# Moving the modulation sums of a transformer block's attention stage from VectorE to ScalarE and GpSimd

## The chip, the cores and the metric

The kernel runs on one core of a Trainium2 chip. The metric is the device time of one launch in microseconds; the time before is 2897.89 us, the median of three runs. The engines are named PE (TensorE), DVE (VectorE), ACT (ScalarE), POOL (GpSimd) and SP (SyncE, which here only issues transfers).

## The reference

Two transformer blocks follow each other on x of 1024 tokens by 1024 channels in float32. The change touches the first one's attention stage:

```python
cond = jax.nn.silu(c)
mod = jnp.einsum('bd,de->be', cond, w_ada[i]) + b_ada[i]
sh1, sc1, gt1, sh2, sc2, gt2 = jnp.split(mod, 6, axis=-1)
h = _rmsnorm(x, g_mix[i]) * (1.0 + sc1) + sh1
q, k, v, qi, ki, wi, cu = jnp.split(h @ w_in[i], split_at, axis=-1)
attn_out = _dsa_attention(q, k, v, qi, ki, wi)   # top 256 keys by an index score, causal
conv_out = _conformer_conv(cu, ...)              # 31 taps, layer norm, silu
x = x + gt1 * (jnp.concatenate([attn_out, conv_out]) @ w_out[i])
# then an MLP of width 4096 modulated with sh2, sc2 and gt2, and the second block
```

Each query keeps the 256 keys with the highest index score. `mod` is a vector-matrix product of a 1024-vector with a 1024 x 6144 matrix.

## The kernel before, in words

Every float32 matmul is made of three: each operand is split into a rounded high part and a low rest (`h_hi`, `h_lo`; `w_hi`, `w_lo`; `q_hi`, `q_lo`), and the products hi*hi, hi*lo and lo*hi are summed in PSUM. Weights come by SP's transfers into four buffers `raw`, in a fixed order (`slots`); a buffer is filled again once a semaphore says that its last user is done.

All engines run one list written by hand, `MICRO`, each taking from it the entries that concern it, in order. The attention stage is 64 slots: 8 query tiles `t` of 128 tokens, 8 heads each; slot `n` is 8t + head. Per slot PE makes the scores (two heads at a time), the transposes of the probabilities two slots back (`turn`) and the product with the values four slots back (`values`). DVE adds the mask to the scores and takes the row maximum (`mask`, line 1503), ACT takes the exponential (line 995) and copies the transposed probabilities out of PSUM (line 987).

The other work of the block is spread over the same slots:

- `conv`: the 31-tap depthwise convolution, as matmuls with diagonal matrices. There are 8 units of 31 taps; `UNIT_SLOTS` gives the slots in which each runs and `taps_by(n)` the taps done by slot n. POOL builds the diagonals three taps at a time (line 662), in two buffers; it waits until PE has used those of two groups earlier. PE takes three matmuls per tap (lines 2099 to 2101).
- `topk`: for query tile 4, DVE finds the 256 highest scores in 32 rounds of eight (lines 1367 and 1369).
- `sel_pass` and `sel_step`: for query tiles 5 to 7, the 256th score is found by bisection of its bits. A pass on ACT counts the scores above a candidate (three `Sign` operations with an accumulator, line 934); a step on DVE makes the next candidate from it (four operations on 3 elements, lines 1388 to 1398). The step of a pass stands one slot after it. `sel_fin` then turns the scores of a tile into a mask on DVE, in six parts, and has to be done before that tile's first slot.
- `ada`: the products for the four parts of `mod` that are used after attention. Each of 32 items takes a 128 x 1024 piece of `w_ada` in `raw`, multiplies it by a column of silu(c) and adds it to one of the sums `gate_sum` or `mlp_sum`. This is one DVE operation (line 1524, or 1527 for a part's first item without bias). `ADA_SLOTS` puts item i at slot 8i // 5. `ada_sum` counts them; it frees the `raw` buffer, and PE's `modsum` (slot 46) and `gate` (slots 57 and 58) wait for it.
- `ln_...`: the layer norm of the convolution, at slots 26 to 42 for the first half of the tokens and at slots 62 and 63 and behind the loop for the second. Its last step is `ln_silu` (line 1573).
- `split_q`: POOL's split of q, once per tile; `wsplit`: POOL's split of the first two pieces of `w_out`, at slots 60 and 62.

After slot 63 a hand-written tail follows with the last values and turns, the division by the row sums (`divide`, line 1538), `ln_silu`, the first matmuls of the output projection (`mixed`: part 0 or 1 for each of four token tiles) and the last rounding to `h_hi` and `h_lo`. There is no scheduler at run time; only the order of the list and the semaphores set what waits for what.

Of the kernel before, what the change touches and what calls it, by code (L numbers as in the profile page):

```python
# [6 lines left out]
ALU = mybir.AluOpType  # L7
ACT = mybir.ActivationFunctionType
# [8 lines left out]
NT = S // P  # L17
NK = D // P
# [5 lines left out]
NH, NKV, HD = 8, 2, 64  # L24
# [21 lines left out]
SEL_TILES = IDX_TILES[3:]  # L46
# [22 lines left out]
def build(nc, a, out):  # L69
    with ExitStack() as ctx:  # L70
        sems = {}

        def sem(name):
            if name not in sems:
                sems[name] = ctx.enter_context(nc.semaphore(name))
            return sems[name]
# [183 lines left out]
        M_OUT = len(used)  # L260
# [136 lines left out]
        TOPK_Q, TOPK_K, TOPK_LAST = 40, 52, 12  # L397
        TOPK_SLOTS = {4: range(0, 31)}
        SEL_EARLY, SEL_ROUNDS = 8, 4
        SEL_AT = {n: SEL_EARLY + k for k, n in enumerate(n for n in range(32) if n % 4 < 3)}  # L400
        FIN_SLOTS = {}
        for ti, at_slots in zip(SEL_TILES, (range(32, 38), range(39, 45), range(46, 52))):
            for part, n in enumerate(at_slots):
                FIN_SLOTS[n] = [("sel_fin", ti, part)]
        UNIT_SLOTS = (0, 6, 12, 18, 24, 34, 42, 52, 62)

        def taps_by(n):

            n = min(n, UNIT_SLOTS[-1])
            u = max(m for m in range(2 * NCC) if UNIT_SLOTS[m] <= n)  # L410
            n0, n1 = UNIT_SLOTS[u], UNIT_SLOTS[u + 1]
            return CONV_K * u + -(-CONV_K * (n - n0) // (n1 - n0))
# [6 lines left out]
        N_ADA = 4 * NK  # L419
        ADA_SLOTS = {8 * i // 5: i for i in range(N_ADA)}  # L420
        GATE_SLOTS = {46: [("modsum", 0, 0)], 57: [("gate", 0, 0), ("gate", 0, 1)], 58: [("gate", 1, 0), ("gate", 1, 1)]}
        WSPLIT_SLOTS = {60: 0, 62: 1}
        MICRO = [("split_q", 0, 0), ("split_q", 1, 0)]
        for t in range(NT):
            for i in range(0, NH, 2):
# [3 lines left out]
                last, older = ([(s // NH, s % NH) for s in (NH * t + i - d, NH * t + i - d + 1)] for d in (2, 4))  # L429
                n = NH * t + i  # L430
                taps = [taps_by(n), taps_by(n) + (taps_by(n + 2) - taps_by(n)) // 3, taps_by(n + 2)]
                for e in range(2):
# [8 lines left out]
                    if n - 1 in SEL_AT:  # L441
                        MICRO.append(("sel_step", SEL_AT[n - 1], 0))
                    if taps[e + 1] > taps[e]:
                        MICRO.append(("conv", taps[e], taps[e + 1]))
                    if n in WSPLIT_SLOTS:
# [12 lines left out]
                    if n in ADA_SLOTS:  # L458
                        MICRO.append(("ada", ADA_SLOTS[n], 0))
                    MICRO += GATE_SLOTS.get(n, [])  # L460
        assert len(SEL_AT) == SEL_PASSES - SEL_EARLY
        assert TOPK_K + TOPK_LAST == 2 * ROUNDS
        assert taps_by(NT * NH) == 2 * NCC * CONV_K
        MICRO += [("values", NT - 1, NH - 4), ("turn", NT - 1, NH - 2), ("values", NT - 1, NH - 3), ("turn", NT - 1, NH - 1),
                  ("mixed", 0, 0), ("mixed", 0, 1), ("ln_gate", 1, 0), ("values", NT - 1, NH - 2), ("values", NT - 1, NH - 1), ("divide", NT - 1, 0),
                  ("ln_silu", 1, 0)]
        MICRO += [("mixed", 0, t) for t in range(2, 4)] + [("out", NT - 1, 0)]
        MICRO += [("ln_hi", 0, 0), ("ln_lo", 0, 0), ("ln_hi", 1, 0), ("ln_lo", 1, 0)]
# [85 lines left out]
        def _(pool):  # L554
# [55 lines left out]
            for n, (kind, _, (n1, n2)) in enumerate(slots):  # L610
# [23 lines left out]
                if m == M_OUT:  # L634
# [13 lines left out]
                    for kind, t, i in MICRO:  # L648
                        tok = slice(t * P, (t + 1) * P)
                        if kind == "split_q" and t >= 2:  # L650
                            split_q(t)
# [139 lines left out]
        def _(act):  # L791
# [184 lines left out]
            for kind, t, i in MICRO:  # L976
# [20 lines left out]
                if kind == "sel_pass":  # L997
                    sel_pass(t, sel_out)
                if kind == "out":
                    u = tp_of[t, "o"]  # L1000
                    act.wait_ge(sem("tp_full"), tp_count[u])
                    s.activation(h_hi[:, 0:4, t * P:(t + 1) * P], ps[:, 4 + u % 2, :].rearrange("p (c q) -> p c q", q=P),
                                 ACT.Copy).then_inc(sem("attn_hi"), 1)
# [214 lines left out]
        def _(dve):  # L1218
# [274 lines left out]
            for kind, t, i in MICRO:  # L1493
# [18 lines left out]
                if kind == "topk":  # L1512
                    topk(t, i)
                if kind == "ada":
                    part, k = t // NK, t % NK
                    acc = (gate_sum[0], mlp_sum[0], mlp_sum[1], gate_sum[1])[part]
                    n = 2 * NK + M_OUT + t
                    dve.wait_ge(raw_in[n % 4], 16 * (n // 4 + 1))
                    if k:
                        dve.wait_ge(sem("ada_sum"), t)  # L1520
                    elif part in (0, 3):
                        dve.wait_ge(sem("gate_bias"), 32)
                    if k or part in (0, 3):
                        v.scalar_tensor_tensor(acc, raw[:, n % 4, :], csil[:, k:k + 1], acc, ALU.mult,
                                               ALU.add).then_inc(sem("ada_sum"), 1)
                    else:
                        v.tensor_scalar(acc, raw[:, n % 4, :], csil[:, k:k + 1], None, ALU.mult).then_inc(sem("ada_sum"), 1)
                if kind == "sel_step":
# [869 lines left out]
```

## Time and profile before

| what | value |
|---|---|
| median of 3 runs | 2897.89 us (2894.88 to 2903.49) |
| the profiled execution, its own time | 2897.89 us |
| its span, first to last instruction | 2896.0 us |
| PE busy | 2707.7 us, 93% |
| DVE busy | 1670.2 us, 58% |
| ACT busy | 759.5 us, 26% |
| POOL busy | 1150.2 us, 40% |
| attention stage, slots 0 to 63 | about 340 to 697 us |

Busy time is the time in which the engine has at least one instruction under way; for PE the ends of matmuls are modelled. An engine's idle time matters only where it is the one that the others wait for. The granted clock is the share of TensorE's full 2.4 GHz that it got; 0.5 is 1.2 GHz.

### The profile page before, as it was taken

The page shows a single profiled execution, that of the slowest core. Times are in us where ns is not written, and L with a number is a line of the kernel's source. Part 1 is how long each engine was busy: PE and PEld are TensorE (multiplying, and loading weights), DVE is VectorE, ACT ScalarE, POOL GpSimd, SP SyncE. Part 2 cuts the span into 40 slices and gives each one's busy share as a digit, 9 for nine tenths or more (in the row PEclk, how much of TensorE's full clock was granted, in tenths as well). Part 3 has the DMA queues.
Part 4 walks back from the last instruction along what each step waited for, and adds up shares of the span by engine and source line. Part 5 has one row for each costly group of instructions (what it writes and reads, how often), then busy time and mean ns, then how long its engine had stood idle before and what let it go on. Part 6 is the DMA issues. An engine that isn't in the chain of part 4 may idle for free.

```text
span 2896.0 us, 34615 instructions
## 1 busy us (share of the span) xinstructions
PE 2707.7 (93%) x13488; PEld 2240.6 (77%) x13488; DVE 1670.2 (58%) x2150; ACT 759.5 (26%) x1314; POOL 1150.2 (40%) x764
## 2 busy tenths in 40 slices
PE   4999988998999999999999999788799999999998
PEld 4867776887878888888876677677688888888887
DVE  6268988855475566665675782455526334444335
ACT  4235477434231001111023442222214000111002
POOL 2422464533454354354342223333364334334332
PEclk8999999999999999999999999899999999999999
DMA  6201021212311111111122110000231111111111
GB/s 217 66 12 33 30 73 51 62 34 76 106 59 42 46 58 43 44 58 38 54 73 67 43 37 15 1 1 1 78 105 59 37 51 58 36 51 58 36 51 58
DMA packets 142488, 153.33 MB, mean 53 GB/s; under 512 B 7183, under 2 KB 105252, under 8 KB 142374
## 3 DMA queue, kind: packets, MB, share of 16 engines
q1 hardware_dynamic: 136512, 141.87, 15.5%
q10 hardware_dynamic: 5862, 9.89, 0.9%
q8 instruction: 77, 1.26, 0.2%
q14 instruction: 37, 0.30, 0.0%
HBM read 143.35 MB, written 8.39 MB: 52 GB/s over the span
## 4 chain that ended last, share of the span: by engine, by line
PE 78%; DVE 12%; ACT 4%; issue 3%; POOL 1%; DMA 1%; ACTq 0%; SPq 0%; DVEq 0%; POOLq 0%
PE ps L1920 11%; PE ps L1905 11%; PE ps L1922 11%; PE ps L1921 11%; PE ps L1907 11%; PE ps L1906 11%; PE ps L2301 4%; ACT sel_out L934 2%; DVE yt L1742 2%; PE ps L2073 2%; PE ps L1996 2%; DVE yt L1731 1%; DVE score L1369 1%; DVE best L1367 1%; PE ps L2063 1%
## 5 line engine op out<-in xcount | busy, mean ns | idle before, releaser
L1905 PE MATMUL ps<-h_hi,w_hi 128*128 128x512 f32 x1472 | 585.3, 398 | 10.1 <-issue 5.6
L1906 PE MATMUL ps<-h_lo,w_hi 128*128 128x512 f32 x1472 | 575.0, 391 | 0.0
L1907 PE MATMUL ps<-h_hi,w_lo 128*128 128x512 f32 x1472 | 575.0, 391 | 0.0
L681 POOL TENSOR_TENSOR w_hi<-raw,zero 128x1024 fp32r<-128x1024 f32 x128 | 243.7, 1904 | 780.2 <-PE ps L1907 397.3
L1920 PE MATMUL ps<-w_hi,u_hi 128*128 128x512 f32 x1024 | 399.1, 390 | 0.0
L1922 PE MATMUL ps<-w_hi,u_lo 128*128 128x512 f32 x1024 | 398.8, 389 | 0.0
L1921 PE MATMUL ps<-w_lo,u_hi 128*128 128x512 f32 x1024 | 398.8, 389 | 0.0
L1060 ACT ACTIVATE act_r<-ps 128x512 f32<-128x512 f32 x128 | 76.4, 597 | 1130.8 <-PE ps L1907 1130.8
L1626 DVE TENSOR_TENSOR act_r<-act_r 128x512 f32<-128x512 f32 x128 | 167.6, 1309 | 328.8 <-ACT act_r L1060 328.6
L684 POOL TENSOR_TENSOR w_lo<-raw,w_hi 128x1024 fp32r<-128x1024 f32 x128 | 338.1, 2642 | 10.1
L1905 PEld LDWEIGHTS ps<-h_hi,w_hi 128*128 128x128 f32 x1472 | 277.9, 189 | 77.6 <-issue 17.6
L1906 PEld LDWEIGHTS ps<-h_lo,w_hi 128*128 128x128 f32 x1472 | 278.0, 189 | 59.9 <-issue 3.7
L1907 PEld LDWEIGHTS ps<-h_hi,w_lo 128*128 128x128 f32 x1472 | 277.6, 189 | 58.4
L1631 DVE TENSOR_TENSOR u_lo<-act_r,u_hi 128x512 fp32r<-128x512 f32 x128 | 226.8, 1782 | 0.0
L1920 PEld LDWEIGHTS ps<-w_hi,u_hi 128*128 128x128 f32 x1024 | 192.7, 188 | 39.9
L1921 PEld LDWEIGHTS ps<-w_lo,u_hi 128*128 128x128 f32 x1024 | 192.6, 188 | 39.9
L1922 PEld LDWEIGHTS ps<-w_hi,u_lo 128*128 128x128 f32 x1024 | 192.5, 188 | 40.1
L1920 PE MATMUL ps<-w_hi,h_hi 128*128 128x512 f32 (+2 forms) x512 | 185.4, 362 | 26.7 <-DVE h_lo L1578 8.5
L1639 DVE TENSOR_TENSOR x<-x,ps 128x512 f32<-128x512 f32 x128 | 88.0, 687 | 212.2 <-PE ps L1922 212.2
L1922 PE MATMUL ps<-w_hi,h_lo 128*128 128x512 f32 (+2 forms) x512 | 183.8, 359 | 0.0
L1921 PE MATMUL ps<-w_lo,h_hi 128*128 128x512 f32 (+2 forms) x512 | 183.8, 359 | 0.0
L1646 DVE TENSOR_TENSOR x<-x,tmp 128x512 f32<-128x512 f32 x128 | 155.0, 1211 | 4.4
(420 smaller groups left out, 4205.5 us busy)
## 6 DMA issues: line engine op xcount, KB each, us to landing
raw<-in_w_up_dram SPq DMA_DIRECT2D x64, 512.0 KB, 4.0
raw<-in_w_down_dram SPq DMA_DIRECT2D x64, 512.0 KB, 3.3
raw<-in_w_ada_dram SPq DMA_DIRECT2D x48, 512.0 KB, 3.7
raw<-in_w_in_dram SPq DMA_DIRECT2D x32, 512.0 KB, 3.7
raw<-in_w_out_dram SPq DMA_DIRECT2D x32, 512.0 KB, 3.2
x<-in_x_dram SPq DMA_DIRECT2D x8, 512.0 KB, 10.7
x<-in_x_dram ACTq DMA_DIRECT2D x8, 512.0 KB, 9.3
x_mid<-x SPq DMA_DIRECT2D x8, 512.0 KB, 5.5
```

The lines of the kernel that those rows point to most:

```text
L681: g_.tensor_tensor(w_hi[:, r, :], raw[:, r, :], zero.to_broadcast([P, 1024]), ALU.add).then_inc(sem("w_hi_done"), 1)
L684: g_.tensor_tensor(w_lo[:, r, :], raw[:, r, :], w_hi[:, r, :].bitcast(F32), ALU.subtract).then_inc(sem("split_done"), 1)
L1626: v.tensor_tensor(act_r[:, b % 4, :], act_r[:, b % 4, :], act_r[:, b % 4, :], ALU.mult).then_inc(sem(f"u_sq{k}"), 1)
L1631: v.tensor_tensor(u_lo[c // 4][:, c % 4, :], act_r[:, c % 4, :], u_hi[c // 4][:, c % 4, :].bitcast(F32), ALU.subtract).then_inc(sem(f"u_lo ...
L1646: v.tensor_tensor(x[:, t, cols], x[:, t, cols], tmp2[:, n % 2, :], ALU.add).then_inc(sem(f"x_sum{k}"), 1)
L1905: mm(ps[:, bank, :], wh, h_hi[:, k, cols], start=(k == 0), stop=False)
L1906: mm(ps[:, bank, :], wh, h_lo[:, k, cols], start=False, stop=False)
L1907: last = mm(ps[:, bank, :], wl, h_hi[:, k, cols], start=False, stop=(k == NK - 1))
L1920: mm(o, hi[:, k0 + k, tok], wh, start=(start and k == 0), stop=False)
L1921: mm(o, hi[:, k0 + k, tok], wl, start=False, stop=False)
L1922: last = mm(o, lo[:, k0 + k, tok], wh, start=False, stop=(stop and k == 1))
L2301: last = mm(out[:, h, :], lhs[:, h, :], rhs[:, h, :], start=True, stop=True)
```

## The change

The `ada` item is split in two. ACT multiplies the piece in place in `raw` (`ada`, at the same slot as before, behind the slot's `sel_pass`), and POOL adds it to the sum three slots later (`ada_add`, `ADA_LAG` = 3; a copy instead of an addition for the two items that begin a part without bias). DVE has no part in it any more. Four tables of the list change as well: `topk` has 24 slots instead of 31, the selection passes stand in two of three slots up to 34 instead of three of four up to 30, `sel_fin` stands in other slots, and the taps of two neighbouring slots are split evenly instead of one third to two thirds. In the tail the first two `mixed` entries move behind the last values, the division and `ln_silu`.

```diff
-        TOPK_SLOTS = {4: range(0, 31)}
+        TOPK_SLOTS = {4: range(0, 24)}
         SEL_EARLY, SEL_ROUNDS = 8, 4
-        SEL_AT = {n: SEL_EARLY + k for k, n in enumerate(n for n in range(32) if n % 4 < 3)}
+        SEL_AT = {n: SEL_EARLY + k for k, n in enumerate(n for n in range(36) if n % 3 < 2)}
         FIN_SLOTS = {}
-        for ti, at_slots in zip(SEL_TILES, (range(32, 38), range(39, 45), range(46, 52))):
-            for part, n in enumerate(at_slots):
-                FIN_SLOTS[n] = [("sel_fin", ti, part)]
+        for ti, at_slots in zip(SEL_TILES, (range(35, 39), range(41, 47), range(48, 54))):
+            for part in range(6):
+                FIN_SLOTS.setdefault(at_slots[part * len(at_slots) // 6], []).append(("sel_fin", ti, part))
...
+        ADA_LAG = 3
...
-                taps = [taps_by(n), taps_by(n) + (taps_by(n + 2) - taps_by(n)) // 3, taps_by(n + 2)]
...
-                    if taps[e + 1] > taps[e]:
-                        MICRO.append(("conv", taps[e], taps[e + 1]))
+                    if taps_by(n + 1) > taps_by(n):
+                        MICRO.append(("conv", taps_by(n), taps_by(n + 1)))
...
                         MICRO.append(("ada", ADA_SLOTS[n], 0))
+                    if n - ADA_LAG in ADA_SLOTS:
+                        MICRO.append(("ada_add", ADA_SLOTS[n - ADA_LAG], 0))
...
-                  ("mixed", 0, 0), ("mixed", 0, 1), ("ln_gate", 1, 0), ("values", NT - 1, NH - 2), ("values", NT - 1, NH - 1), ("divide", NT - 1, 0),
+                  ("ln_gate", 1, 0), ("values", NT - 1, NH - 2), ("values", NT - 1, NH - 1), ("divide", NT - 1, 0),
                   ("ln_silu", 1, 0)]
-        MICRO += [("mixed", 0, t) for t in range(2, 4)] + [("out", NT - 1, 0)]
+        MICRO += [("mixed", 0, t) for t in range(4)] + [("out", NT - 1, 0)]
...
+                        if kind == "ada_add":
+                            part, k = t // NK, t % NK
+                            acc = (gate_sum[0], mlp_sum[0], mlp_sum[1], gate_sum[1])[part]
+                            r = (2 * NK + M_OUT + t) % 4
+                            pool.wait_ge(sem("ada_prod"), t + 1)
+                            if k:
+                                pool.wait_ge(sem("ada_sum"), t)
+                            elif part in (0, 3):
+                                pool.wait_ge(sem("gate_bias"), 32)
+                            if k or part in (0, 3):
+                                g.tensor_tensor(acc, acc, raw[:, r, :], ALU.add).then_inc(sem("ada_sum"), 1)
+                            else:
+                                g.tensor_copy(acc, raw[:, r, :]).then_inc(sem("ada_sum"), 1)
...
+                if kind == "ada":
+                    n = 2 * NK + M_OUT + t
+                    act.wait_ge(raw_in[n % 4], 16 * (n // 4 + 1))
+                    s.activation(raw[:, n % 4, :], raw[:, n % 4, :], ACT.Copy,
+                                 scale=csil[:, t % NK:t % NK + 1]).then_inc(sem("ada_prod"), 1)
...
-                if kind == "ada":
-                    part, k = t // NK, t % NK
-                    acc = (gate_sum[0], mlp_sum[0], mlp_sum[1], gate_sum[1])[part]
-                    n = 2 * NK + M_OUT + t
-                    dve.wait_ge(raw_in[n % 4], 16 * (n // 4 + 1))
-                    if k:
-                        dve.wait_ge(sem("ada_sum"), t)
-                    elif part in (0, 3):
-                        dve.wait_ge(sem("gate_bias"), 32)
-                    if k or part in (0, 3):
-                        v.scalar_tensor_tensor(acc, raw[:, n % 4, :], csil[:, k:k + 1], acc, ALU.mult,
-                                               ALU.add).then_inc(sem("ada_sum"), 1)
-                    else:
-                        v.tensor_scalar(acc, raw[:, n % 4, :], csil[:, k:k + 1], None, ALU.mult).then_inc(sem("ada_sum"), 1)
```

## Rows read from the trace of the kernel before

**Rows 1.** The page's first line.

```profile
span 2896.0 us, 34615 instructions
```

**Rows 2.** Stage by windows: us; busy PE, PEld, DVE, ACT, POOL; clock; DMA share, GB/s.

```profile
340.00:462.55 122.55, 110.45 (x583) 88.37 (x583) 104.39 (x240) 87.68 (x185) 81.66 (x92) 1.00 0.21 65
462.55:512.03 49.48, 42.54 (x203) 32.13 (x202) 41.30 (x93) 37.51 (x68) 17.49 (x18) 0.89 0.17 54
512.03:553.86 41.83, 40.74 (x254) 33.66 (x253) 32.90 (x57) 17.24 (x37) 25.05 (x24) 0.97 0.21 64
553.86:697.00 143.14, 139.78 (x912) 116.83 (x911) 77.17 (x126) 61.70 (x115) 53.87 (x54) 0.98 0.11 34
```

**Rows 3.** Who waited for whom, 340 to 462.55: total us, times, longest.

```profile
POOL diag_hi L662 <- PE ps L2101: 41.9, 32, 3.6
...
DVE sel_acc L1388 <- ACT sel_out L934: 12.5, 18, 1.6
...
PE ps L1996 <- DVE smax L1503: 8.8, 7, 1.8
...
PE ps L2099 <- POOL diag_lo L662: 1.4, 3, 0.6
```

**Rows 4.** PE's waits, 340 to 697.

```profile
PE ps L1996 <- DVE smax L1503: 14.1, 11, 2.4
```

**Rows 5.** Timeline around two waits: start us, us, instruction, idle before it.

```profile
480.50 0.71 PE L1996 MATMUL ps<-k_hi,q_hi 64*128 64x512 f32 x2 [2.40 <-DVE smax L1503]
...
504.67 1.28 DVE L1524 SCALAR_TENSOR_TENSOR scale_sum<-raw,csil,scale_sum 128x1024 f32<-128x1024 f32 x1
505.87 0.68 DVE L1503 CUSTOM_DVE_ANT_0 prob<-ps,score 128x512 f32<-128x512 f32 x1
...
506.66 0.49 PE L1996 MATMUL ps<-k_hi,q_hi 64*128 64x512 f32 x2 [3.38 <-issue]
```

**Rows 6.** DVE's groups, 340 to 462.55: busy us, mean ns, idle before.

```profile
L1367 DVE MAX8 best<-score 128x8 f32<-128x640 f32 x24 | 19.8, 825 | 0.6
L1369 DVE MATCH_REPLACE8 score<-best,score 128x640 f32<-128x640 f32 x24 | 19.4, 809 | 0.0
L1524 DVE SCALAR_TENSOR_TENSOR gate_sum<-raw,csil,gate_sum 128x1024 f32<-128x1024 f32 x8 | 11.0, 1377 | 0.3
...
L1390 DVE TENSOR_TENSOR sel_low<-sel_low,sel_pick 128x3 f32<-128x3 f32 x18 | 7.9, 438 | 0.6
```

**Rows 7.** POOL's groups by form: whole span, and (last row) 340 to 462.55.

```profile
L580 POOL TENSOR_TENSOR w_lo<-raw,w_hi 128x1024 fp32r<-128x1024 f32 x28 | 71.2, 2544 | 2.2
...
L578 POOL CAST w_hi<-raw 128x1024 fp32r<-128x1024 f32 x28 | 31.0, 1107 | 131.4 <-PE ps L1907 59.4 <-PE ps L1922 44.7 <-PE ps L2073 27.2
...
L662 POOL TENSOR_TENSOR diag_lo<-ident,cw_lo 128x384 fp32r<-128x384 f32 x40 | 38.6, 966 | 0.0
```

**Rows 8.** ACT's groups, whole span.

```profile
L934 ACT ACTIVATE sel_out<-score,sel_cand,sel_sign 128x768 f32<-128x768 f32 (+2 forms) x72 | 81.6, 1134 | 18.4 <-DVE sel_cand L1398 12.1 <-DVE sel_cand L1396 1.8
...
L811 ACT ACTIVATE junk<-x 128x1024 f32<-128x1024 f32 x48 | 50.6, 1055 | 155.2 <-DVE x L1594 50.2 <-DVE x L1603 40.3 <-DVE x L1639 33.4
...
L934 ACT ACTIVATION_READ_ACCUMULATOR sel_out<-score,sel_cand,sel_sign 128x1 f32 x72 | 13.4, 186 | 0.0
```

**Rows 9.** Line 1573 in 560:570 and in 700:715: ns min/median/max, first and last start.

```profile
L1573 DVE TENSOR_TENSOR conv<-conv,squares x4: 682/684/685, 564.6 to 566.4; 128x512 f32<-128x512 f32 x4
...
L1573 DVE TENSOR_TENSOR conv<-conv,squares x4: 951/2201/2894, 704.4 to 709.5; 128x512 f32<-128x512 f32 x4
```

**Rows 10.** Busy time and granted clock of one stretch.

```profile
507.90:514.80 6.90, 6.90 (x29) 6.32 (x29) 6.62 (x11) 1.68 (x5) 1.01 (x2) 0.51 0.12 49
```

**Rows 11.** Timeline of the stage's end.

```profile
700.02 3.68 PE L2073 MATMUL ps<-vtok,probT 128*128 128x64 f32 x32
...
703.79 0.69 DVE L1538 TENSOR_TENSOR otok<-ps,srec 128x512 f32<-128x512 f32 x1 [2.56 <-issue]
...
720.94 0.76 PE L1920 MATMUL ps<-w_hi,h_hi 128*128 128x512 f32 x1 [8.48 <-DVE h_lo L1578]
```

More of the change, by code:

```diff
@@ L429, in build @@
                 last, older = ([(s // NH, s % NH) for s in (NH * t + i - d, NH * t + i - d + 1)] for d in (2, 4))
-                n = NH * t + i
-                taps = [taps_by(n), taps_by(n) + (taps_by(n + 2) - taps_by(n)) // 3, taps_by(n + 2)]
                 for e in range(2):
```

## The prediction

> **What bounds the kernel now.** I read the page first, for the span [rows 1], and then cut the attention stage into stretches with the table by windows [rows 2]. A slot is one (query tile, head) step of the stage, eight to a tile, and I place its start at its mask operation on DVE. Slots 0 to 23 are 340.0 to 462.55 us, slots 24 to 31 are 462.55 to 512.03, slots 32 to 39 are 512.03 to 553.86, and slots 40 to 63 with the last heads run to 697. The reader is to see that PE is busy in nearly all of it: 333.5 of 357.0 us, so 23.5 us of idle time is all that any relief of another engine can give back, plus what a slower clock costs. From 553.86 on PE is idle for 3.4 of 143.1 us, so work moved there or taken from there is worth almost nothing.
>
> In slots 0 to 23 the chain of waits [rows 3] says which queue is late. DVE is busy 104.4 us of 122.55 [rows 2] and waits 12.5 us for ACT's selection passes, all of them at the first operation of a `sel_step`; it has no other slack. PE waits 8.8 us for a mask that stands behind other work in DVE's queue. ACT is busy 87.7 us, POOL 81.7 us, and POOL waits 41.9 us until PE has used a pair of diagonals. So PE and DVE are nearly level, ACT and POOL have room.
>
> In slots 24 to 31 PE's idle time is 6.9 us [rows 2]. Over the whole stage 14.1 us of its waits end with a mask [rows 4]; in this tile the longest two [rows 5] end with the masks of slots 27 (2.4 us) and 31 (3.38 us, given as issue, but it ends as the mask of slot 31, which begins at 505.87). Ahead of that mask DVE does a 1.28 us `ada` step. The granted clock was 0.51 from 507.9 to 514.8 [rows 10], right after the second of them, and a like stretch of 6.9 us began at 480.6, right after the first.
>
> **The change part by part.**
>
> *DVE loses the ada steps.* Slots 0 to 23 hold 15 of the 32 (items 0 to 14). Of the 14 fused ones eight are the gate_sum row at 1.38 us [rows 6] and six the like operation on shift_sum, at about the same; with the first item of shift_sum, a plain product of about 1 us, 20.8 us leave DVE.
>
> *DVE gets the selection by eights earlier.* All 32 rounds of tile 4 now lie in slots 0 to 23; there were 24. A round is 0.825 + 0.809 + 0.09 us for the value load between them = 1.73 us [rows 6], so 8 more cost 13.8 us here, and leave slots 24 to 30.
>
> *Selection passes get thinner.* 24 passes stood in slots 0 to 30 (18 of them in 0 to 23); now 16 stand in 0 to 23, 6 in 24 to 31, 2 in 33 and 34. A step on DVE is four operations of three elements; the row of `sel_low` gives 0.438 us each, the other three 0.31 to 0.43, 1.52 us a step. Two fewer save 3.0 us of DVE. A pass on ACT is three of 1.13 us with accumulator reads of 0.186 us [rows 8] = 4.0 us; two fewer save 8 us of ACT.
>
> *ACT gets 32 products of 128x1024.* The nearest row is 1.055 us [rows 8], the upper bound 1.24 us for Sign at that size. 15 of them are 15.8 us, less the 8 us: ACT stands at 95.5 of 122.5 us. In slots 24 to 31 it is 37.5 us busy and gets 5 x 1.06 = 5.3 us: 42.8 of 49.5. Behind a product on ACT stand the next slot's copy of `probT` and its exponential, for which PE's turn two slots later waits; that lead is about 10 us, so 1.06 us is hidden unless ACT has a backlog.
>
> *POOL gets 30 additions and 2 copies.* The nearest row is the subtraction of 128x1024 at 2.54 us; a copy is 1.11 us [rows 7]. In slots 0 to 23 fall 14 (items 0 to 13, three slots late), 13 x 2.54 + 1.1 = 34.1 us, which uses 81% of the 41.9 us that POOL waits. What is queued behind an addition is the next pair of diagonals, 2 x 0.97 us at most [rows 7]; POOL can be two pairs ahead, six taps of three matmuls, about 4 us of PE work, and an addition with one pair is 4.5 us. That is nearly covered by the scores, values and turns between. Where POOL's own splitting of q (2.3 us, every eighth slot) meets an addition, PE waits about 1 us. The loads into `raw` are released three slots later than before, 15 us, with four buffers and 1.6 slots to an item; the transfer still has over 10 us.
>
> *What the two engines do to each other.* POOL's large operations hold up a DVE operation that reads two operands from SBUF: `conv * squares` takes 0.68 us alone and 0.95 to 2.89 us beside POOL's 2.5 us splits [rows 9]. In `sel_step` the effect is there now: four operations of 0.161 us at least take 0.38 us on average, 0.22 us more each, beside diagonals of 0.9 us. With POOL busier and a third of its time in operations of 2.5 us, each of 64 operations takes from nothing more to, at worst, a whole addition per step, 16 x 2.5 = 40 us. Nearer to what the rows show I take 0.38 instead of 0.22 us, 64 x 0.16 = 10 us. The Trainium skill (SBUF — State Buffer, Who interferes with whom) says that an operation of VectorE with two SBUF inputs and one of GpSimd that reads SBUF exclude each other for the whole instruction. By that rule alone every step could lose a full addition and the gain of this part would be gone; the rows of 0.161 us at the least and 0.38 us on average show that most operations miss POOL's.
>
> Sum for DVE in slots 0 to 23: 104.4 - 20.8 + 13.8 - 3.0 + 10 = 104.4 us. It is as loaded as before, POOL is close to PE, and I count **0 us** for these slots (ends: -6, most of the 8.8 us gone; +12, DVE at 134 us by the worst lock).
>
> *Slots 24 to 31.* Ahead of mask 31 DVE had two rounds (3.5 us), the closing operation and a 1.28 us ada step; all are gone, more than the 3.4 us. Ahead of mask 27 only one round of 1.73 us goes, and the pass that this step waits for comes 1.06 us later behind a product, so 1.1 of 2.4 us is worth counting. **-4.5 us** (ends -7 and 0).
>
> *The clock.* Each of the two slow stretches takes 3.4 us out of PE if it is busy. The second begins 1.2 us after the wait that goes. I count a bit over half of one, **-2.0 us** (ends: both gone -6.9; one more, +3.4).
>
> *Slots 32 on.* `sel_fin` parts move two or three slots later and tile 5's six parts into four slots, about 10 us of DVE work beside 8 us of masks, in 20 us of PE work. Slot 37 takes two parts and the affine step, 8.8 us, but slots 38 and 39 are light and the masks have to be there only by slot 40. The even split of the taps changes the order inside a pair of heads, not its sum. **0 us** (-3 to +3).
>
> *The end.* Before, 12 matmuls of `mixed` (697.4 to 700.2, 2.8 us) stood ahead of the last 32 of values, which end at 703.7; DVE then does `otok` at 703.79 and the four `conv * squares`, and PE later waits 8.48 us until 720.94 for DVE's `h_lo` [rows 11]. The matmuls are now behind the values, in time in which PE has work either way. DVE's affine step ends at 701.1, so the chain starts 2.4 us earlier: **-2.4 us** (ends -2.8 and 0, where POOL's splits, also released earlier, hold it again).
>
> Total: 0 - 4.5 - 2.0 + 0 - 2.4 = -8.9 us. The profiled execution took 2897.89 us with a span of 2896.0, which is the median of the runs shown; the forecast is 2889.0 us.
>
> **The rivals.**
> - *All waits for masks go.* For it: DVE without lock trouble is 94.4 us in slots 0 to 23, and 14.1 us of PE's 23.5 us idle are waits for masks [rows 4]. Against it: POOL at 116 of 122 us and the unknown lock. Then -6 - 6 - 5 - 2.4 = -19.4: 2878.5 us.
> - *PE was the bound anyway, and what DVE gives up ACT and POOL take.* For it: PE 110.5 of 122.55 us busy, ACT in slots 24 to 31 with 42.8 us and a backlog of the layer norm's squares and table loads. Then only the end and a little is left: 2895 us. That is the case in which the change does not do what it says.
> - *Slower: POOL becomes the bound of slots 0 to 23.* Place: the diagonals behind an addition. It decides once an addition with its delays costs more than 41.9 / 14 = 3.0 us; the split that I take as its price went up to 2.73 us without this neighbourhood. If PE then waits 1.1 us at each of the 14, +15 us; less the 2.4 us of the end and 4.5 us of slots 24 to 31: 2906 us. Against it: DVE's operations of 1.3 us that hold POOL up today (pairs stretched to 1.8 us) go.
>
> **How the numbers follow.** Forecast, 2881 to 2895: 0.45. All waits gone, near 2878.5: 0.17. Hidden, 2895 to 2899: 0.20. POOL or the lock decides, over 2900: 0.18. 0.3% of 2897.9 is 8.7 us, about what a measurement of this kernel can tell from no change. The line is at 2889.2, so 0.27 of the forecast's 0.45 counts as faster: faster 0.44, same 0.18 + 0.20 = 0.38, slower 0.18. The range leaves out half of the slower case and a part of the first rival: 2877 to 2904.
>
> **What would show it.** In the profile after: no `ada` rows on DVE, 32 ACT products of about 1.06 us and 30 POOL additions near 2.5 us. PE's waits for masks in slots 24 to 31 should fall from 7 us to about 2, with one slow clock stretch fewer there; slots 0 to 23 should stay within 3 us of 122.5. The wait ahead of `h_lo` should fall from 8.5 to 6. I am wrong if PE's waits for `diag_lo` in slots 0 to 23 (1.4 us now) rise over 8 us, if the small `sel_step` operations average over 0.8 us, or if ACT's backlog makes DVE wait for passes more than the 12.5 us of now.

## The result: 36 us slower

The changed kernel takes 2937.17 us (median of 4 runs, 2935.9 to 2938.01), the kernel before 2900.69 us in the same comparison (4 runs, 2894.88 to 2905.19). The ratio is 1.0127, with a 95% interval of 1.0106 to 1.0147: 1.27% or 36.5 us slower, where 2889 us was forecast and 2904 was the upper end.

The page of the changed kernel, its span, busy times and granted clock in 40 slices:

```profile
span 2937.2 us, 34646 instructions
...
PE 2728.3 (93%) x13488; PEld 2257.2 (77%) x13488; DVE 1668.0 (57%) x2118; ACT 791.9 (27%) x1346; POOL 1208.2 (41%) x796
...
PEclk8999998889999999999999999899999999999999
```

Between the two profiled executions the span grew by 41.2 us. PE has the same 13488 matmuls and is busy 20.6 us longer (2707.7 before). So half of the growth is matmuls at a lower clock and half is idle PE. DVE's sum has hardly moved (1670.2 before) although 32 items left it: other DVE operations became about as much longer.

Windows of the changed kernel, cut at the masks of slots 24, 32 and 40 as in [rows 2], then at 646 and at 741, which is 8.2 us behind the last mask, as 697 was before:

```profile
339.70:489.60 149.90, 123.52 (x597) 98.51 (x595) 113.90 (x242) 95.67 (x188) 107.66 (x110) 0.92 0.16 50
489.60:536.70 47.10, 42.93 (x206) 32.72 (x207) 21.21 (x53) 39.00 (x67) 23.63 (x23) 0.86 0.18 57
536.70:592.40 55.70, 44.11 (x238) 36.66 (x237) 39.90 (x68) 32.45 (x61) 30.67 (x27) 0.82 0.15 48
592.40:646.00 53.60, 50.65 (x301) 43.97 (x300) 32.64 (x48) 22.76 (x41) 31.41 (x25) 0.84 0.16 50
646.00:741.00 95.00, 93.47 (x612) 76.07 (x611) 44.57 (x74) 46.67 (x82) 41.75 (x37) 1.00 0.09 29
```

| part of the stage | before | after | forecast | measured |
|---|---|---|---|---|
| slots 0 to 23 | 122.55 | 149.90 | 0 | +27.4 |
| slots 24 to 31 | 49.48 | 47.10 | -4.5 (clock -2.0) | -2.4 |
| slots 32 to 39 | 41.83 | 55.70 | 0 | +13.9 |
| slots 40 to 63 and on | 143.14 | 148.60 | 0 | +5.5 |
| wait at the end | 8.48 | 5.82 | -2.4 | -2.7 |

The measured column sums to 41.7, close to the 41.2 us by which the span grew. The waits of slots 0 to 23, beside [rows 3]:

```profile
POOL diag_hi L676 <- PE ps L2106: 45.3, 22, 8.6
...
DVE sel_acc L1407 <- ACT sel_out L948: 21.8, 15, 2.1
...
PE ps L2001 <- DVE smax L1522: 17.8, 4, 6.3
PE ps L2104 <- POOL diag_lo L676: 7.7, 8, 3.2
```

PE now waits four times for a mask in place of seven, but 17.8 us in place of 8.8, up to 6.3 us each. It waits 7.7 us for diagonals in place of 1.4. POOL itself waits for PE for 45.3 us of this longer stretch, so over the whole of it POOL is not the bound, though in single places it is late by up to 3.2 us. DVE waits 21.8 us for passes although fewer of them stand here.

**One long wait, instruction by instruction.** The timeline of the changed kernel ahead of the mask of slot 9 (start us, us, instruction, idle before it): first DVE, then POOL, then PE.

```profile
386.66 1.67 DVE L1407 TENSOR_TENSOR sel_acc<-sel_sum,sel_rank 128x3 f32<-128x3 f32 x1 [1.50 <-ACT sel_out L948]
388.37 0.76 DVE L1408 TENSOR_TENSOR sel_pick<-sel_acc,sel_cand 128x3 f32<-128x3 f32 x1
389.16 0.76 DVE L1409 TENSOR_TENSOR sel_low<-sel_low,sel_pick 128x3 f32<-128x3 f32 x1
389.94 0.75 DVE L1417 SCALAR_TENSOR_TENSOR sel_cand<-sel_base,sel_low 128x3 f32<-128x3 f32 x1
390.73 0.83 DVE L1386 MAX8 best<-score 128x8 f32<-128x640 f32 x1
...
393.46 0.81 DVE L1388 MATCH_REPLACE8 score<-best,score 128x640 f32<-128x640 f32 x1
394.30 0.42 DVE L1522 CUSTOM_DVE_ANT_0 prob<-ps,cmask 128x256 f32<-128x256 f32 x1
...
385.91 2.41 POOL L661 TENSOR_TENSOR gate_sum<-gate_sum,raw 128x1024 f32<-128x1024 f32 x1
388.26 0.84 POOL L676 TENSOR_TENSOR diag_hi<-ident,cw_hi 128x384 fp32r<-128x384 f32 x1
389.05 0.84 POOL L676 TENSOR_TENSOR diag_lo<-ident,cw_lo 128x384 fp32r<-128x384 f32 x1
...
394.88 0.58 PE L2001 MATMUL ps<-k_hi,q_hi 64*128 64x256 f32 x2 [6.29 <-DVE smax L1522]
```

Read the ends. The addition on POOL ends at 388.32, and DVE's operation on three elements, begun 1.7 us earlier, ends at 388.33. The diagonals end at 389.10 and 389.89, DVE's next operations at 389.13 and 389.92. Each small operation lasts until the POOL operation beside it is over, so a step costs four POOL operations, 4.0 us here, and it has POOL's backlog ahead of it because an addition has just held the diagonals up. Behind the step stand two rounds of `topk` (390.73 to 394.27), then the mask that PE waits 6.29 us for. Two rounds in one slot come in every third slot (32 rounds in 24 slots), and it is always a slot with a step. Slots 3, 9, 15 and 21, each right behind such a slot, are the four waits, 17.8 us together. Slots 6, 12, 18 and 24 stand behind such a slot too, but PE does not wait at them for a mask: it takes the scores two heads at a time, and all its waits for masks here end at the second mask of a pair.

The same in the kernel before, with POOL idle until 378.19, and two slots on with POOL at work:

```profile
376.78 0.16 DVE L1388 TENSOR_TENSOR sel_acc<-sel_sum,sel_rank 128x3 f32<-128x3 f32 x1 [0.42 <-ACT sel_out L934]
376.98 0.16 DVE L1389 TENSOR_TENSOR sel_pick<-sel_acc,sel_cand 128x3 f32<-128x3 f32 x1
...
384.77 0.76 DVE L1389 TENSOR_TENSOR sel_pick<-sel_acc,sel_cand 128x3 f32<-128x3 f32 x1
...
378.19 0.83 POOL L662 TENSOR_TENSOR diag_hi<-ident,cw_hi 128x384 fp32r<-128x384 f32 x1 [3.31 <-PE ps L2101]
...
384.68 0.83 POOL L662 TENSOR_TENSOR diag_hi<-ident,cw_hi 128x384 fp32r<-128x384 f32 x1
```

The price is thus one of two: 0.16 us, or the rest of a POOL operation. Counted over the timeline of slots 0 to 23, 31 of 73 operations on 128x3 elements took over 0.2 us before, and all 31 end within 0.1 us of the end of a POOL operation; after the change it is 40 of 65, and all 40 end so. The mean of all rose from 0.38 to 0.62 us.

**Slot 35** is the longest piece of what slots 32 to 39 lose. It holds the last step and two parts of `sel_fin`, 13 small operations and two large ones. On POOL two additions and the end of a third, a split of q and four pairs of diagonals run beside them. Timeline of the changed kernel, DVE, POOL, PE:

```profile
560.00 2.31 DVE L1423 TENSOR_TENSOR sel_step<-sel_next,sel_value 128x3 f32<-128x3 f32 x1
...
568.07 2.26 DVE L1442 SCALAR_TENSOR_TENSOR sel_kth<-sel_exact,sel_sign 128x1 f32<-128x1 f32 x1
570.37 0.82 DVE L1522 CUSTOM_DVE_ANT_0 prob<-ps,score 128x640 f32<-128x640 f32 x1
...
559.90 2.40 POOL L661 TENSOR_TENSOR scale_sum<-scale_sum,raw 128x1024 f32<-128x1024 f32 x1
...
567.98 2.34 POOL L661 TENSOR_TENSOR scale_sum<-scale_sum,raw 128x1024 f32<-128x1024 f32 x1
...
574.01 1.08 PE L2086 MATMUL ps<-ident,otok 128*128 128x128 f32 x4 [7.00 <-ACT probT L1001]
```

The last step alone takes 555.42 to 564.70, 9.3 us. In the kernel before the same ten operations took 506.66 to 508.60, 1.9 us, with POOL idle. The mask of slot 36 comes at 570.37, and PE waits 7.00 us in one piece: the copy of `probT` that it needs stands in ACT's queue behind the exponential of slot 36, and that waits for the mask. POOL's additions are not all of this loss: with the same tables and `ada` on DVE (below) slots 32 to 39 are already 12.1 us longer.

**The clock after such waits**, in two windows of the changed kernel (columns as in [rows 2]), the first right behind the wait of 6.29 us, the second around the wait of 7.00 us:

```profile
394.80:402.00 7.20, 7.12 (x31) 6.12 (x32) 4.77 (x15) 6.86 (x14) 1.62 (x2) 0.70 0.00 0
569.00:580.00 11.00, 5.99 (x30) 5.28 (x31) 9.15 (x17) 4.13 (x8) 1.32 (x1) 0.54 0.16 48
```

0.50 is the lower of the two levels, 1.2 GHz, and a mean between 0.5 and 1 is a window that holds some of both. This is what [rows 10] showed before after a wait of 3.38 us. All ten waits of PE of 2.2 us or more in the changed kernel's stage, the one of 3.2 us for diagonals among them, were followed by 7 us at 0.50 to 0.78; two waits of 1.7 and 1.8 us in the kernel before (ending at 364.69 and 376.32) left it at 1.00. Over slots 0 to 23 the clock fell from 1.00 to 0.92, over slots 32 to 39 from 0.97 to 0.82. In the 5.5 us of the slots from 40 on is a wait of 2.9 us for POOL's split of q, which stands behind an addition of 2.82 us.

**The end.** One row of PE's timeline, beside the last of [rows 11]:

```profile
762.38 0.77 PE L1925 MATMUL ps<-w_hi,h_hi 128*128 128x512 f32 x1 [5.82 <-DVE h_lo L1583]
```

### The profile page after: what moved, and what is told of

It is laid out like the page before. It is cut to its first block, busy times and chain, and to the rows that moved or that the text cites. A ratio compares the mean times of both kernels' runs of the same rounds, so it can differ in the third digit from the quotient of the medians.

```text
span 2937.2 us, 34646 instructions
## 1 busy us (share of the span) xinstructions
PE 2728.3 (93%) x13488; PEld 2257.2 (77%) x13488; DVE 1668.0 (57%) x2118; ACT 791.9 (27%) x1346; POOL 1208.2 (41%) x796
## 3 DMA queue, kind: packets, MB, share of 16 engines
q8 instruction: 77, 1.26, 0.2%
## 4 chain that ended last, share of the span: by engine, by line
PE 79%; DVE 10%; ACT 4%; issue 3%; POOL 3%; DMA 1%; ACTq 0%; SPq 0%; DVEq 0%; POOLq 0%
PE ps L1925 11%; PE ps L1926 11%; PE ps L1927 11%; PE ps L1910 11%; PE ps L1912 10%; PE ps L1911 10%; PE ps L2306 4%; PE ps L2078 2%; DVE yt L1747 2%; PE ps L2001 1%; ACT sel_out L948 1%; DVE yt L1736 1%; PE ps L2104 1%; PE ps L2105 1%; PE ps L2106 1%
```

## The experiments

Each was compared with the kernel before. Percentages are the ratio's; intervals are 95%.

### Which part of the change costs

**Only the split of `ada`** (ACT product, POOL addition three slots later), no table changed:

```diff
+                    if n - ADA_LAG in ADA_SLOTS:
+                        MICRO.append(("ada_add", ADA_SLOTS[n - ADA_LAG], 0))
```

> The kernel before with only the ada items split into an ACT product and a POOL addition three slots later; all slot tables, the tap split and the tail as before. Theory L (POOL's additions stretch the small sel_step operations on DVE, and PE waits for masks behind them): 10 to 30 us slower than before, sel_step operations over 0.55 us on average in slots 0 to 23, more slow-clock stretches. Theory G (the cost is in the new slot tables, which put a step and two topk rounds ahead of one mask): within 5 us of before or faster, up to 8 us. Theory P (POOL is the bound): slower by over 10 us with PE's waits for diag_lo over 8 us.

2924.79 us, +0.78% (0.60 to 0.96): about 23 us. Slots 0 to 23 take 135.2 us (122.5 before); the small operations take 0.57 us on average.

**Only the shorter `topk`** (`TOPK_SLOTS = {4: range(0, 24)}`):

> The kernel before with only topk packed into slots 0 to 23. DVE still has the ada steps, so slots 0 to 23 get 13.8 us more of DVE work on an engine with 104.4 of 122.55 us busy and 12.5 us of waits. Theory G: 10 to 25 us slower, PE waits in slots 0 to 23 for masks of slots behind a double round. Theory L: under 5 us slower, since without POOL's additions the step is short.

2899.56 us, -0.04% (-0.15 to +0.07). Slots 0 to 23 take 8.1 us longer (130.6) and slots 24 to 63 4.2 us less.

**Only the selection's slots** (`SEL_AT` over 36 slots, `FIN_SLOTS` from 35):

> The kernel before with only the new slots of the selection passes (two of three up to 34) and of sel_fin. Theory G: about 5 us slower, by slot 35 that holds the last step and two parts of sel_fin. Theory L: within 4 us of before, since the last step's 12 small operations take 2 us when POOL is idle.

2899.3 us, 0.00% (-0.11 to +0.11).

**All tables and the tail, `ada` whole on DVE**:

> The changed kernel with the ada items back on DVE as one operation: all new tables, the even tap split and the new tail stay. Theory G: as slow as the changed kernel or slower, 30 us and more over before. Theory L: not over 10 us slower than before, so that the move accounts for most of the 36 us.

2920.54 us, +0.60% (0.43 to 0.77): about 17 us with no addition on POOL at all. POOL's load can't be the reason here; two tables that cost nothing each must cost together, or the two small edits cost.

By stretches, in us more than before, cut at the same masks:

| | slots 0 to 23 | 24 to 31 | 32 to 39 | 40 to 63 and on |
|---|---|---|---|---|
| only the split of `ada` | +12.7 | +3.2 | +6.0 | +4.1 |
| all tables and the tail, `ada` on DVE | +12.4 | -8.6 | +12.1 | +4.4 |
| the changed kernel | +27.4 | -2.4 | +13.9 | +5.5 |

So slots 0 to 23 lose about equally by both parts, and slots 32 to 39 more by the tables than by the additions.

**`topk` in 24 slots and the selection's slots, nothing else**:

> The kernel before with both the topk slots (24) and the selection slots (36, with sel_fin), nothing else. Each alone cost nothing, the even split alone cost 4.6 us, all tables with the new tail cost 17.5 us. Theory G (every third slot holds a sel_step and two topk rounds ahead of one mask): 8 to 15 us slower, with PE's waits behind slots 3, 9, 15 and 21. Rival C (it takes the even split to make late masks felt): within 4 us of before.

2915.04 us, +0.52% (0.36 to 0.69), about 15 us, against 0 and 0 for each alone. Before, two rounds came once in 31 slots; now they meet a step every third slot. Slots 0 to 23 take 132.4 us and slots 32 to 39 53.2 us (41.8 before), where the ten operations of slot 35's step take 4.8 us (532.51 to 537.28) with no addition on POOL. Why slots 32 to 39 lose so much more here than with the selection's slots alone (45.9 us) is not shown.

**As all tables, but the double round moved to the slot without a step**:

```diff
-                            MICRO += [("topk", ti, r) for r in range(ROUNDS * done // of, ROUNDS * (done + 1) // of)]
+                            MICRO += [("topk", ti, r) for r in range(-(-ROUNDS * done // of), -(-ROUNDS * (done + 1) // of))]
```

> All new tables, even split and new tail, ada steps on DVE (the run that was 17.5 us slower), with one edit: the double round of topk falls into slots 0, 3, 6 and so on, which have no sel_step. The sum of work is the same. Theory G: at least 8 us faster than with the double round in slots 2, 5, 8. Rival (the density of topk as such): the same 17.5 us.

2902.59 us, +0.09% (0.00 to 0.19). The same work in the same stage, one round placed a slot away, and 0.51 points of the 0.60 are gone.

**The changed kernel with that one line**:

> The changed kernel with the double rounds of topk in the slots without a sel_step. If the parts add up: 36.5 less the 15 us that this edit gave without the ada move, 20 to 25 us over before. If the lock and the grouping are one and the same loss (DVE's queue ahead of a mask): over 28 or under 15.

2917.8 us, +0.56% (0.39 to 0.73), so 0.71 points or 20 us less than the change. In slots 0 to 23 the wait at slot 9 falls from 6.29 to 4.50 us and that at slot 21 from 3.12 to 0.56:

```profile
PE ps L2001 <- DVE smax L1522: 10.4, 5, 4.5
```

**Only the even split of the taps**, and **the changed kernel with the old split**:

```diff
-                    if taps[e + 1] > taps[e]:
-                        MICRO.append(("conv", taps[e], taps[e + 1]))
+                    if taps_by(n + 1) > taps_by(n):
+                        MICRO.append(("conv", taps_by(n), taps_by(n + 1)))
```

> The kernel before with only the even split of the taps. The tables without the ada move were 17.5 us slower, while topk alone and the selection slots alone cost nothing. Theory C (the even split leaves PE 1.1 us less of taps behind a pair's second turn, so that each late mask is felt): 8 to 18 us slower. Rival (topk and selection slots together put the step and the double round in one slot): within 3 us of before.

> The changed kernel with the split of the taps of before, one third ahead of a pair's second turn and two thirds behind it. The even split alone cost 4.6 us. If that cost only adds up: 32 us over before instead of 36. If the split multiplies what late masks cost (PE has 1.1 us less of work behind the second turn, and each wait may bring a slow-clock stretch): 20 to 28 us over before. Theory L: over 20 us slower in each case.

Alone 2904.84 us, +0.16% (0.06 to 0.25). In the changed kernel it makes no difference: 2936.85 us with the old split, +1.28% (1.11 to 1.45).

**Only the tail** (the two `mixed` entries moved):

> The kernel before with only the two mixed entries moved behind the last values. The prediction's step: 2.4 us faster (0.1%), the wait ahead of DVE's h_lo falls from 8.5 to about 6 us. Rival: POOL's splits start earlier too and hold the four conv operations as before, 0 to 1 us.

2893.78 us, -0.20% (-0.29 to -0.12), 12 runs: faster than both kernels and the fastest of the versions that compute everything. Its wait is that of the changed kernel:

```profile
717.44 0.77 PE L1920 MATMUL ps<-w_hi,h_hi 128*128 128x512 f32 x1 [5.83 <-DVE h_lo L1578]
```

**A version built on this**: the tail, and `topk` in 25 slots with its double rounds where no step stands, `ada` on DVE:

> The kernel before with the new tail (5.6 us faster alone) and topk in slots 0 to 24, its double rounds in the slots 0, 4, 8 to 24, which hold no sel_step there. Theory G: the waits behind slots 27 and 31 get shorter since slots 25 to 30 lose their rounds, and nothing is lost before: 8 to 14 us faster than before. Rival: only the tail's 5 to 6 us.

2900.1 us, +0.02% (-0.07 to +0.11). It missed. Slots 0 to 23 take 129.3 us and slots 24 to 63 226.3 (226.1 before): the time that the earlier rounds cost did not come back later.

### Why the split of `ada` costs

**The kernel before with idle work added**, at the slots of items 0 to 14 or three slots later: 15 ACT copies of 128x1024; 13 POOL additions of 128x1024 with a memset; 14 POOL memsets of 128x2048, which read nothing. The semaphores are left out here and in the next edits:

```diff
+ s.activation(relu[:, 0, :], score[7], ACT.Copy, scale=0.5)                   # ACT
+ g.tensor_tensor(relu[:, 0, :], relu[:, 0, :], relu[:, 1, :], ALU.add)        # POOL, reads
+ g.memset(relu[:, 0:2, 0:1024], 0.0)                                          # POOL, only writes
```

> The kernel before, with its ada steps on DVE, plus 15 idle ACT operations of 128x1024 (a scaled copy of scores into memory that is free then), at the slots of the changed kernel's products in slots 0 to 23. The last run of the ada split alone was 22.6 us slower, DVE waited 27.0 instead of 12.5 us for selection passes. Theory ACT (the product delays exponentials and the next pass, DVE stands at the step's wait, masks come late): 8 to 15 us slower, DVE's wait for passes well over 12.5 us. Theory L (the lock by POOL's additions): within 3 us of before.

> The kernel before, with its ada steps on DVE, plus 13 idle POOL additions of 128x1024 that read two operands, and one memset, at the slots of the changed kernel's first 14 additions. Theory L: over 10 us slower, sel_step operations at 0.55 us or more. Theory ACT: under 5 us slower.

> The same with 14 POOL memsets of 128x2048, which take about as long (2 us) but read nothing. Theory L in its strict form (a POOL operation that reads holds up a DVE operation with two inputs): 5 us or more faster than the run with additions, sel_step operations near 0.38 us as before. If only POOL's queue matters (late diagonals): as slow as the run with additions.

ACT: 2902.73 us, +0.07% (-0.05 to +0.18). POOL reading: 2928.35 us, +0.99% (0.70 to 1.29). POOL writing: 2900.42 us, 0.00% (-0.15 to +0.14). The groups of slots 0 to 23, first with additions, two answers for DVE and for POOL:

```profile
L1402 DVE TENSOR_TENSOR sel_pick<-sel_acc,sel_cand 128x3 f32<-128x3 f32 x18 | 17.4, 967 | 0.6
L1537 DVE SCALAR_TENSOR_TENSOR gate_sum<-raw,csil,gate_sum 128x1024 f32<-128x1024 f32 x8 | 14.4, 1798 | 0.3
...
L660 POOL TENSOR_TENSOR relu<-relu 128x1024 f32<-128x1024 f32 x13 | 32.0, 2463 | 0.0
```

then with memsets:

```profile
L1399 DVE TENSOR_TENSOR sel_pick<-sel_acc,sel_cand 128x3 f32<-128x3 f32 x18 | 7.1, 393 | 0.6
L1534 DVE SCALAR_TENSOR_TENSOR gate_sum<-raw,csil,gate_sum 128x1024 f32<-128x1024 f32 x8 | 11.4, 1420 | 0.3
...
L657 POOL MEMSET relu<- 128x2048 f32 x14 | 25.3, 1809 | 0.0
```

25.3 us more on POOL cost nothing, 33.8 us (with the one memset of 1.8) that read two operands cost 28 us. The two are not equally long, but a third more time would hardly lead from 0 to 28 us: the reading is the price, not POOL's busy time as such. It is paid by DVE's large operations too: its own `ada` steps take 1.80 us beside the additions and 1.42 beside the memsets. The changed kernel has no such steps, so these 28 us are not the price of its additions. The Trainium skill (SBUF — State Buffer, Who interferes with whom) has this rule, and the trace agrees: 0.39 us for `sel_pick` beside writes, 0.97 beside reads.

**Each addition cut in four of 256 columns** (only the split of `ada`):

```diff
+  for q in range(4):
+      w = slice(256 * q, 256 * (q + 1))
+      g.tensor_tensor(acc[:, w], acc[:, w], raw[:, r, w], ALU.add)
```

> The ada split alone (22.6 us slower than before), with each POOL addition cut into four of 128x256, about 0.6 us each. Theory L by length (a small DVE operation stands for the rest of one POOL instruction, so 2.4 us ones are what hurts): 8 us or more of the 22.6 come back, and the longest sel_step operation falls from over 2 us to about 1. Theory L by share (POOL reads without a break, each of the four operations of a step waits for whatever instruction runs): within 5 us of the uncut run.

2927.49 us, +0.93% (0.76 to 1.10). The small operations fall from 0.57 to 0.49 us, and the time does not: POOL is busier (108.7 us in slots 0 to 23 where it was 103.3). PE's waits over the stage say where the time goes, first with the additions whole, then in quarters:

```profile
PE ps L2003 <- DVE smax L1524: 16.9, 5, 5.3
PE ps L2106 <- POOL diag_lo L678: 12.5, 8, 3.7
```

```profile
PE ps L2109 <- POOL diag_lo L681: 21.4, 10, 4.2
PE ps L2006 <- DVE smax L1527: 6.6, 2, 4.6
```

The late masks become fewer and the late diagonals more. With the additions whole, PE's waits for diagonals have already grown from 4.1 us before to 12.5, more than those for masks (14.1 before); 10.0 of the 12.5 us lie behind slot 23. POOL's queue is thus a second price of the split of `ada`, beside the one that DVE pays.

**The ada operation on DVE shrunk to a copy of one column** (30 of the 32 items), which leaves the modulation sums out; then the same with the 15 idle ACT copies, and with the 13 idle POOL additions:

```diff
-   v.scalar_tensor_tensor(acc, raw[:, n % 4, :], csil[:, k:k + 1], acc, ALU.mult, ALU.add)
+   v.tensor_copy(acc[:, 0:1], raw[:, n % 4, 0:1])
```

> The kernel before with DVE's ada steps cut to a copy of one column (30 of 32 items; the modulation sums are left out), nothing added on ACT or POOL. It bounds what taking the steps off DVE can give. The prediction's view: PE's waits behind slots 27 and 31 and part of the 8.8 us in slots 0 to 23 go, 8 to 20 us faster than before. Rival W (what DVE saves it spends at the sel_step, waiting for ACT's pass): under 5 us faster, DVE's wait for passes up from 12.5 to over 20 us.

> The same with the 15 idle ACT products of 128x1024 in slots 0 to 23. With DVE's steps in place the products cost nothing. Rival W: once DVE waits for passes, what delays them counts: 3 to 10 us slower than the run without products. Theory L: within 3 us of it.

> The same with the 13 idle POOL additions and one memset in slots 0 to 23 and no products. With DVE's steps in place they cost 28 us. Theory L with sel_step as the place: 15 us or more over the run without additions, and over before. If the 28 us came mainly from DVE's own ada steps meeting POOL's additions (both read two operands): under 10 us.

Shrunk: 2898.13 us, -0.04% (-0.15 to +0.07). With ACT copies: 2894.82 us, -0.19% (-0.30 to -0.09). With POOL additions: 2903.26 us, +0.13% (-0.01 to +0.26).

The first of them is the main reading. DVE loses nearly the full cost of `ada` (it is busy 87.6 us in slots 0 to 23, 104.4 before), nothing is added anywhere, and the kernel is not faster. One row of its waits in slots 0 to 23, where [rows 3] has 12.5 us:

```profile
DVE sel_acc L1388 <- ACT sel_out L934: 24.4, 18, 2.1
```

What DVE no longer does, it mostly waits: the step stands one slot behind its pass, and the pass is not earlier. The windows of slots 0 to 23, first shrunk, then with the additions:

```profile
339.64:463.46 123.82, 113.76 (x584) 92.31 (x583) 87.62 (x239) 87.65 (x185) 72.87 (x92) 0.96 0.21 65
```

```profile
339.36:472.18 132.82, 116.81 (x583) 93.80 (x582) 98.50 (x239) 87.64 (x185) 103.92 (x106) 0.94 0.19 60
```

The additions make slots 0 to 23 9.0 us longer, with DVE 10.9 us busier; in this profile slots 24 to 63 are 5.1 us shorter than in the other (217.6 and 222.7), and the medians differ by 5.1 us. What was expected for "under 10 us" has come: most of the 28 us that the same additions cost on the kernel before goes with DVE's own `ada` steps. These met the additions themselves, and they left DVE less time to make up for late steps; which of the two counted more is not separated. What the changed kernel pays in slots 0 to 23 is the smaller part, by the small operations: the kernel with only the split takes 135.2 us there, this one 132.8, the shrunk one 123.8, so the additions alone make 9.0 of the 11.4 us between them.

## Why the prediction was wrong

- **"Sum for DVE in slots 0 to 23 ... I count 0 us": this step failed, in two ways.** The sum was too small: DVE is busy 113.9 us, not 104.4. The small operations took 40.4 us (65 of 0.62), not 64 x 0.54 = 34.6, and the closing operation of `topk` (2.45 us) moved in with the rounds and was left out; these are 8.3 of the 9.5 us. Above all a sum over 24 slots was the wrong measure. PE waits for one mask, and what counts is what stands ahead of it. A step and a double round together make the mask behind them late, 17.8 us in four waits, while DVE waits elsewhere. The runs show it with the sum unchanged: +0.60% with the two together, +0.09% one slot apart; in the changed kernel 1.27% and 0.56%.
- **"DVE loses the ada steps": worth nothing with the tables of before.** The 20.8 us left, and without any new work nothing was gained (-0.04%). DVE's wait for passes took up most of them (12.5 to 24.4 us). What the freed time is worth with the new tables was not run. The rival "PE was the bound anyway" was right in this part. The Trainium skill (Perfetto Trace Analysis, Optimizing Scalar/DVE Operations) warns that work moved between VectorE and GpSimd might not help, because of the shared port; here it cost.
- **"What the two engines do to each other": right mechanism, wrong form and place.** 10 us was counted as a mean; it is all or nothing, and an addition also piles up the diagonals behind it, so that the following operations of the step meet one each. The worst end for slots 0 to 23 (+12) was below what they lost (+27.4). A place I did not look at, for this price or any other, was slot 35 with the last step and two parts of `sel_fin`: "0 us (-3 to +3)" for slots 32 to 39 became +13.9, of which the tables alone make 12.1.
- **"ACT gets 32 products": costs nothing**, as forecast; one takes 1.14 us, and 15 idle ones change the time by +0.07% on the kernel before and by -0.15 points on the shrunk one.
- **"Slots 24 to 31, -4.5"**: PE's idle time there fell from 6.9 to 4.2 us and the stretch by 2.4. But it was paid by the rounds moved into slots 0 to 23: alone, +8.1 there and -4.2 later.
- **"The clock, -2.0": wrong sign.** I gave the gain of a wait that goes, not the loss of waits that come. PE's busy time rose by 20.6 us, half of the loss.
- **"The end, -2.4": right.** The wait went from 8.48 to 5.82 us. Alone the tail is worth 0.20%, 5.7 us; its wait accounts for 2.6 of them, and where the rest comes from is not shown.
- **The rival for slower, "POOL becomes the bound"**, had the sign and a part of the cause: in slots 0 to 23 PE's waits for `diag_lo` rose by 6.3 us to 7.7, just below the 8 that were named and well below the 17.8 for masks. With only the split of `ada` the waits for diagonals grow more than those for masks, but behind slot 23 (10.0 us, 2.7 before). Of the three signs named for a wrong forecast, the small operations stayed at 0.62 (0.8 was named) and only the wait for passes (21.8 over 12.5) came true.

By parts, from the ratios: the split of `ada` +0.78, the two tables together +0.52, the even split +0.16, the tail -0.20, in sum +1.26 against 1.27 measured. The agreement is partly luck, since the even split costs nothing in the changed kernel.

What stays open: the split of `ada` costs 0.78%, while its pieces on the kernel without ada on DVE (nothing -0.04%, products a further -0.15 points, additions of the first 14 items +0.17 points) make far less. In slots 0 to 23 they account for most of it (9.0 of 11.4 us). The other 18 items, whose additions stand in slots 25 to 52, were not in these runs, and slots 24 to 63 are 13.5 us longer in the run with the split only; there PE waits 10.0 us for diagonals. Whether this is the additions alone, or product and addition together, was not separated. Nor is it shown why the regrouped version gave nothing back.

## What to carry to other kernels

When work moves between queues, don't compare sums over a stage: list for each late hand-over (here each mask) what stands ahead of it in its queue, and look for periods of two tables that fall together. Before moving work off an engine, shrink that work to nothing and time it; if the kernel is no faster, the move by itself has nothing to win. Price a GpSimd operation that reads SBUF by what it does to VectorE's two-operand operations beside it, the small ones above all, and by what it holds up in GpSimd's own queue. Here each wait of TensorE of 2.2 us or more was paid again in the clock.

## What was not expected of the hardware

A VectorE operation on 128x3 elements took 0.16 us or lasted to the end of the GpSimd operation beside it, up to 2.31 us beside an addition of 2.40; the long ones are not noise, since all 40 end within 0.1 us of the end of a GpSimd operation. Three operations with one tensor input and as few elements (`TENSOR_SCALAR`, 128x3) were held up in slot 35 as well, 0.76 to 0.77 us in place of 0.17; another on 128x1 took its usual 0.16 us in the middle of an addition (554.51). A GpSimd addition of 128x1024 took 2.39 us, a memset of 128x2048 1.81 us, and the latter cost the kernel nothing. The price of idle TensorE is twofold: over the stage 23 us more idle time came with 21 us more busy time for the same matmuls.
